# A pad of 384 bytes ahead of the raw weights and a 1,024-byte constants buffer: where the on-chip buffers begin

## What is computed

```
x = first_block(x, ...)      # two layers: attention, then a convolutional feed-forward
#   x = x + attention(rmsnorm(x)) @ w_o
#   x = x + (silu(gate) * val) @ w_down,  gate, val = conv(rmsnorm(x) @ w_up)
x = second_block(x, ...)     # one hybrid layer
#   proj = rmsnorm(x) @ w_in
#   oa = chunk_gated_delta_rule(...);  ob = chunk_retention(...)
#   x = x + rmsnorm((sigmoid(ga) * (oa @ w_br_a) + sigmoid(gb) * (ob @ w_br_b)) @ w_out)
#   x = x + rmsnorm(square(relu(rmsnorm(x) @ w_up)) @ w_down)
return x
```

## Time and profile before

| | |
|---|---|
| median of 3 runs | 1304.36 us (1304.25 to 1304.54) |
| span of the profiled execution, first to last instruction | 1302.3 us |
| PE busy in that span | 1294.9 us (99%) |
| weight loads (PEld) busy | 1174.9 us (90%) |
| DVE, ACT, POOL busy | 937.4, 721.9, 89.4 us |
| mean granted TensorE clock | 0.999 of full speed |
| read from main memory | 215.78 MB |

### The profile page before, as it was taken

One profiled execution on the slowest core, in us unless ns is written; L12 is line 12 of the kernel. 1 busy time (PEld: TensorE's weight loads), 2 busy tenths in 40 slices (PEclk: granted clock), 3 DMA queues, 4 the chain that ended last, 5 costly groups with the idle time before them and its releaser, 6 DMA issues.

```text
span 1302.3 us, 23200 instructions
## 1 busy us (share of the span) xinstructions
PE 1294.9 (99%) x9416; PEld 1174.9 (90%) x9416; DVE 937.4 (72%) x1606; ACT 721.9 (55%) x1265; POOL 89.4 (7%) x181
## 2 busy tenths in 40 slices
PE   9999999999999999999999999999999999999998
PEld 8988999998879999989999999878999888989896
DVE  7866887776877977777888888864677655765553
ACT  7555665555666655547666666653444443644442
POOL 1000000000000000000122233300000000000000
PEclk9999999999999999999999999999999999999999
DMA  8443465553424655554444444456544445465530
GB/s 332 162 162 130 162 226 184 176 190 133 159 100 161 226 195 185 176 189 146 135 135 134 135 114 122 143 187 224 202 170 170 163 169 178 181 224 194 187 138 33
DMA packets 35036, 219.26 MB, mean 168 GB/s; under 512 B 4208, under 2 KB 7664, under 8 KB 9456
## 3 DMA queue, kind: packets, MB, share of 16 engines
q1 hardware_dynamic: 30608, 211.83, 45.2%
q10 hardware_dynamic: 4320, 5.94, 2.9%
HBM read 215.78 MB, written 1.05 MB: 166 GB/s over the span
## 4 chain that ended last, share of the span: by engine, by line
PE 97%; DVE 1%; ACT 1%; issue 0%; POOL 0%; ACTq 0%; DVEq 0%; POOLq 0%
PE bank L326 30%; PE bank L327 28%; PE bank L328 28%; PE bank L718 1%; PE bank L769 1%; PE bank L444 1%; PE bank L1756 1%; PE bank L1773 1%; PE bank L790 1%; PE bank L2447 0%; PE bank L712 0%; PE bank L1636 0%; PE bank L580 0%; PE bank L1912 0%; PE bank L1626 0%
## 5 line engine op out<-in xcount | busy, mean ns | idle before, releaser
L326 PE MATMUL bank<-sb_h_hi,sb_w_hi 128*128 128x256 f32 x1504 | 428.0, 285 | 0.4 <-DVE sb_w_lo L319 0.4
L327 PE MATMUL bank<-sb_h_lo,sb_w_hi 128*128 128x256 f32 x1504 | 419.9, 279 | 0.0
L328 PE MATMUL bank<-sb_h_hi,sb_w_lo 128*128 128x256 f32 x1504 | 419.7, 279 | 0.0
L286 DVE TENSOR_TENSOR sb_w_lo<-sb_raw,sb_w_hi 128x1024 fp32r<-128x1024 f32 x185 | 226.3, 1223 | 99.1 <-ACT sb_w_hi L278 98.8
L326 PEld LDWEIGHTS bank<-sb_h_hi,sb_w_hi 128*128 128x128 f32 x1504 | 282.5, 188 | 4.8 <-issue 2.2
L327 PEld LDWEIGHTS bank<-sb_h_lo,sb_w_hi 128*128 128x128 f32 x1504 | 282.1, 188 | 1.7
L328 PEld LDWEIGHTS bank<-sb_h_hi,sb_w_lo 128*128 128x128 f32 x1504 | 282.4, 188 | 0.0
L278 ACT CAST sb_w_hi<-sb_raw 128x1024 fp32r<-128x1024 f32 x188 | 197.1, 1048 | 99.7 <-PE bank L328 97.3
L289 DVE TENSOR_TENSOR sb_w_lo<-sb_raw,sb_w_hi 128x1024 fp32r<-128x1024 f32 x185 | 225.3, 1218 | 0.0
L279 ACT CAST sb_w_hi<-sb_raw 128x1024 fp32r<-128x1024 f32 x188 | 197.7, 1052 | 0.0
L326 PE MATMUL bank<-sb_w_hi,sb_h_hi 128*128 128x256 f32 (+1 forms) x512 | 160.4, 313 | 0.0
(11 more groups left out here) (382 smaller groups left out, 1940.7 us busy)
## 6 DMA issues: line engine op xcount, KB each, us to landing
sb_raw<-stream SPq DMA_DIRECT2D x199, 1024.0 KB, 4.8
sb_row<-rows ACTq DMA_DIRECT2D x3, 512.0 KB, 3.7
sb_x<-x SPq DMA_DIRECT2D x4, 256.0 KB, 4.7
sb_raw<-stream SPq DMA_DIRECT2D x2, 512.0 KB, 6.1
sb_norm_b<-norm_b ACTq DMA_DIRECT2D x4, 256.0 KB, 4.3
out<-sb_x SPq DMA_DIRECT2D x4, 256.0 KB, 2.0
sb_g_row<-sb_g_rows ACTq DMA_DIRECT2D x7, 128.0 KB, 6.3
sb_retain<-retain ACTq DMA_DIRECT2D x1, 768.0 KB, 4.1
```

The lines of the kernel that those rows point to most:

```text
L286: V.tensor_tensor(w_lo[:, b, 0:HALF], raw[:, r, 0:HALF], w_hi[:, b, 0:HALF].bitcast(F32), ALU.subtract).then_inc(lo_done, 1)
L326: T.matmul(out_ap, l_hi, r_hi, start=start, stop=False, **kw)
L327: T.matmul(out_ap, l_hi, r_lo, start=False, stop=False, **kw)
L328: return T.matmul(out_ap, l_lo, r_hi, start=False, stop=stop, **kw)
```

## The change

No instruction is added, removed or moved: on every engine the changed program has the same instructions in the same order with the same waits. What changes is the address of every buffer. A pad of 96 values (384 bytes) that nothing reads or writes goes ahead of `raw`, and `consts` becomes 256 values (1,024 bytes) wide, of which the same 201 are loaded and used.

```diff
+RAW_PAD = 96
+CONST_COLS = 256
...
+        sb("raw_pad", [P, RAW_PAD])
         raw = sb("raw", [P, RAW, UNIT])
...
-        consts = sb("consts", [P, P + 9 * KD + 1])
-        ident, freq = consts[:, 0:P], consts[:, P + 9 * KD:]
+        consts = sb("consts", [P, CONST_COLS])
+        ident, freq = consts[:, 0:P], consts[:, P + 9 * KD:P + 9 * KD + 1]
...
-            A.dma_start(consts[:], a["consts"]).then_inc(consts_in, 16)
+            A.dma_start(consts[:, 0:P + 9 * KD + 1], a["consts"]).then_inc(consts_in, 16)
```

## The result

The changed kernel takes 1316.11 us (median of 4 runs, 1315.87 to 1316.48), beside 1304.33 us of the kernel before in the same comparison: a ratio of 1.0092, 95% interval 1.0080 to 1.0104. It is slower by 11.8 us, on the side to which I had given 17%, and above the upper end of the range (1312).

The account below looks back on a forecast made before the run. The prediction took PE's matmul paces as the bound. Its terms, 0 + 0 + 0 + 0 on a span of 1302.3 us, with 2.0 us around the span, left the median at 1304.4 us; range 1293 to 1312.

Parts of the forecast that it names:

- the side to which I had given 17%: Whole kernel: slower as the short 256-column pace gives way, from 1307 to 1314 us; chance 0.17.
- What bounds the kernel: PE, busy 1294.9 of 1302.3 us: time is the sum of its matmul paces, with hardly any waits.
- Stationary operands, cost 0: PE matmuls: new start addresses of the loaded operands cost 0, bounded under 1 us in all.
- Moving operands: PE matmuls: new addresses of streamed operands cost 0, bounded by a gain of 19.0 us and a loss of 9.2.
- the two paces that the trace shows: 256-column matmuls: a long pace of 0.1181 or 0.1180 us and a short one near 0.1133, 4.7 ns apart.
- The rival that came true: 256-column matmuls: reads at equal offsets interfere, the short pace is lost; 9.2 us slower, 1313.6 us; chance 0.17.
- DVE, ACT, transfers, 0: Engines beside PE and DMA loads: new offsets cost 0; transfers bounded from 0 to -0.4 us.
- The sign that I had named: Kernel head: a first `features` matmul that starts earlier would show that the transfers there gained.
- The rival that only half is announced: Stage buffers behind `small` lose their multiples of 512 or 256; costs nothing, ends within the forecast; no separate chance.
- The first rival: 256-column matmuls: the long pace gives way; all of it 1285.4 us, half 1294.9; chance 0.25.

Follow-up runs that it names:

- `m_lo` apart: Against the kernel with `consts` 304 values wide, `m_lo` buffers moved 64 bytes further on than `m_hi`; one run, 1292.61 us.
- the alternating laps: Feed-forward rounds in the kernel with `consts` 304 values wide plus 16 values of padding behind `mid_lo`; 1296.06 us, ratio 0.9940.
- the table: Kernel before, pad only, changed kernel, and `consts` alone widened to 256, 320, 304, 224, 216 or 248 values; 1293.3 to 1319.9 us.
- 304 values: Against the kernel before, `consts` made 304 values wide, without the pad ahead of `raw`; 1293.32 us, ratio 0.9919.
- 304 values and 48 behind `mid_lo`: Against the kernel before, `consts` 304 values wide and 48 values of padding behind `mid_lo`; 1291.31 us, ratio 0.9903.

## Why the prediction was wrong

**What bounds the kernel** was right. Time is the sum of PE's paces: a change whose waits are no longer than before cost 12.4 us, and the working by classes accounts for it.

**Stationary operands, cost 0: wrong, in the reading of the rows.** I arranged by where the stationary operand begins, 0, 256 and 448, and found one pace. By distance the same four stretches are two cases only, 128 (feed-forward, `m`) and 64 (`mid`, `h`), which cost the same. I counted "differences of 128, 384 and 192 bytes" as three; modulo 256 the first two are one. Putting `mid` and `h` at a distance of 0 took 5.6 and 4.7 ns off each of 864 matmuls, 4.6 us in all, where I had bounded the term at under 1 us.

**Moving operands, "I therefore take 0 here too": this is the step that failed.** Two things went into it. That both paces occur at the same offsets was right, and that a pace depends on more than the stretch's own offsets; the laps with `m_lo` apart and the alternating laps show it. That it is what went before is likely, not shown. But I concluded from it that the offsets matter little. They decide which paces are to be had: at a distance of 0, all 256-column matmuls run at 119.7 ns. The bounds, too, were built from the two paces that the trace shows, with the long one as the worst case. The new pace lies above it, so that the 4,512 `features` matmuls, most of which I had at the worst pace already, lost 10.2 us.

**The rival that came true**, that the short pace gives way because reads at equal offsets get into each other's way, had its direction and its reason from the one combination "that no row shows". Its size was 9.2 us; the 256 columns lost 18.1 us, since the long pace rose as well, and the 512 columns gained 4.6 where I had a loss in the tail. The 9.2 us itself was too high: I read the shares of the paces from durations, 80% of `features` at the long one, while the start-to-start distances (117.4 between 113.4 and 117.8) give some 90%. By them the short pace's loss alone comes to 6.7 us, and the other 11.4 us (6,000 x 1.9 ns) are the step from 117.8 to 119.7, for which the prediction had no term. These errors and the gain of the 512 columns partly cancel; it is luck that they brought the time (1316.1) near the rival's 1313.6. Its mechanism is right in that the relation of the two operands counts; that the distance to the next matmul's load sets the pace is not borne out. And I ended the range at 1312, below that rival's own price: a combination without a row should have been given an end beyond any pace seen.

**DVE, ACT, transfers, 0: right.** The busy times of DVE and ACT are within 0.6 us of before, and the DMA rows after read:

```profile
sb_raw<-stream SPq DMA_DIRECT2D x199, 1024.0 KB, 4.8
...
sb_x<-x SPq DMA_DIRECT2D x4, 256.0 KB, 4.7
...
sb_norm_b<-norm_b ACTq DMA_DIRECT2D x4, 256.0 KB, 4.7
```

`x` at a multiple of 512 lands after 4.7 us as it did at 128, and `norm_b`, at 320 now, after 4.7 instead of 4.3; PE's wait for `x` is the 0.2 us above, and nothing waits for `norm_b`. The Trainium skill's rule on multiples of 256 bytes ("DMA: Bandwidth & Descriptors", "How a descriptor splits into AXI transactions"), which would have made the head 0.5 us shorter, does not show in `x`'s landing; in the time of the kernel with the pad alone (1304.13 against 1304.06, an interval of 0.1% to either side) 0.5 us could not be told. The sign that I had named did come: the first `features` matmul starts at 9.5 us instead of 9.9, and at 9.6 with the pad alone. But in the twelve kernels whose `x` begins at 128, the one before among them, it starts anywhere from 9.5 to 10.1, so that this does not show the rule either. The page speaks of bytes that are "fetched but unused"; what is fetched here lies in main memory, where the change moves nothing.

The other page of the Trainium skill that I weighed ("SBUF — State Buffer", "Specifications (TRN2)", lines of 16 bytes) led the wrong way. All buffers here begin at multiples of 32, so that by that rule, as I read it, every kernel of the table costs the same; they span 1293.3 to 1319.9 us.

**The rival that only half is announced** ended where I said: the feed-forward's buffers and `m`, which lost their multiples of 512 or 256, cost 0.3 us. The first rival, the long pace giving way, did not happen with this change; 304 values brought a part of it.

## What to carry to other kernels

Where PE is the bound and matmuls follow each other without pauses, look at where the streamed operand lies relative to the loaded one, modulo 256 bytes, for each class of matmul; aligning buffers for its own sake can put both at the same place, which cost 256-column matmuls 2 to 6 ns each here and gave 512-column ones 5 to 6 back. Try three or four paddings between the two groups of buffers: it is one number, and here it moved the time from 1319.9 to 1293.3 us, and a second one to 1291.3. And when a row is missing for a combination that a change brings in, take the bounds beyond the rows that there are, to both sides.

## What the runs showed of the hardware that I had not expected

- The same instructions on the same data took 1291.3 to 1319.9 us, 2.2%, by nothing but the distance between buffers. The best padding, 304 values and 48 behind `mid_lo`, is faster than the kernel before by 0.97% (0.82% to 1.11%).
- A 256-column matmul has a pace of 119.7 ns at a distance of 0, and 113.4 or 117.8 at 64 and 192; a 512-column one has some 227 to 228 at 0, 229 to 230 at 192 and 233 at 64, all at a granted clock of 0.999 or 1.0. A distance of 0 is the best for 512 columns, and for 256 columns among the worst.
- The pace of a stretch can depend on more than its own operands, probably on what ran ahead: the same `features` matmuls at the same addresses ran at 117.8 ns in one kernel and 113.5 in another, and in a third the laps took the two paces in turn. A change in one class of matmuls is thus paid or repaid in another, by 1 to 5 us in these runs.
